# The attention loop of a two-layer diffusion block, written out in place of a loop with registers

## The reference, cut to what matters

```python
def attend_block(q_blk):                      # 128 queries at a time
    sc = jnp.einsum("bqhd,bkhd->bhqk", q_blk.astype(jnp.float32), k_all) * scale
    p = jax.nn.softmax(sc, axis=-1)
    return jnp.einsum("bhqk,bkhd->bqhd", p, v_all).astype(q_blk.dtype)
```

## Time and profile before

| what | us |
|---|---|
| median of 3 runs | 2488.7 |
| lowest and highest | 2485.72, 2490.02 |
| the profiled execution, its own time | 2494.57 |
| span of the profiled execution | 2492.7 |

### The profile page before, as it was taken

One profiled execution on the slowest core, in us unless ns is written; L12 is line 12 of the kernel. 1 busy time (PEld: TensorE's weight loads), 2 busy tenths in 40 slices (PEclk: granted clock), 3 DMA queues, 4 the chain that ended last, 5 costly groups with the idle time before them and its releaser, 6 DMA issues.

```text
span 2492.7 us, 32113 instructions
## 1 busy us (share of the span) xinstructions
PE 2418.2 (97%) x11124; PEld 1955.7 (78%) x11124; DVE 1848.6 (74%) x2786; ACT 1208.3 (48%) x1948; POOL 611.2 (25%) x473
## 2 busy tenths in 40 slices
PE   8989999999899999999999899999999999999997
PEld 3868878788788788888888687766887888888886
DVE  4467667677637988888754779998579888887556
ACT  3356656566643544444553442244635454445542
POOL 0057587864042300011000321100432000110002
PEclk9999999999999999999999999999999999999999
DMA  6046465642431455555865567711314555558644
GB/s 269 27 144 174 128 176 161 186 135 68 144 125 65 121 146 147 132 132 140 261 216 172 183 186 180 158 39 46 118 52 127 149 139 135 136 140 275 210 169 170
DMA packets 153204, 366.31 MB, mean 147 GB/s; under 512 B 14433, under 2 KB 15713, under 8 KB 153057
## 3 DMA queue, kind: packets, MB, share of 16 engines
q1 hardware_dynamic: 107056, 242.69, 28.1%
q0 software_dynamic: 44416, 116.93, 21.7%
q10 hardware_dynamic: 1584, 4.85, 0.6%
HBM read 303.07 MB, written 136.31 MB: 176 GB/s over the span
## 4 chain that ended last, share of the span: by engine, by line
PE 75%; DVE 18%; issue 4%; ACT 1%; DMA 1%; POOL 1%; SPq 0%; DVEq 0%; POOLq 0%; ACTq 0%
PE psum L2299 22%; PE psum L2301 22%; PE psum L2300 22%; DVE acts L2209 3%; DVE acts L2211 3%; PE psum L2515 2%; PE psum L2504 1%; PE psum L2505 1%; DVE small L1748 1%; DVE weights_f32r L1848 1%; DVE acts L2213 1%; DMA low<-x_t 1%; PE psum L2613 1%; DVE high_f32r L1966 1%; DVE low L1945 1%
## 5 line engine op out<-in xcount | busy, mean ns | idle before, releaser
L2299 PE MATMUL psum<-acts_f32r,weights_f32r 128*128 128x512 f32 x1536 | 607.8, 396 | 16.0 <-DVE low L2027 6.7
L2301 PE MATMUL psum<-acts_f32r,weights_f32r 128*128 128x512 f32 x1536 | 600.8, 391 | 0.0
L2300 PE MATMUL psum<-acts_f32r,weights_f32r 128*128 128x512 f32 x1536 | 600.2, 391 | 0.0
L955 ACT ACTIVATE weights_f32r<-low 128x512 fp32r<-128x512 f32 (+2 forms) x471 | 303.7, 660 | 447.5 <-DVE low L1994 257.4
L2299 PEld LDWEIGHTS psum<-acts_f32r,weights_f32r 128*128 128x128 f32 x1536 | 289.9, 189 | 80.2 <-DVE low L2027 7.5
L2301 PEld LDWEIGHTS psum<-acts_f32r,weights_f32r 128*128 128x128 f32 x1536 | 289.6, 189 | 61.3
L2300 PEld LDWEIGHTS psum<-acts_f32r,weights_f32r 128*128 128x128 f32 x1536 | 290.0, 189 | 58.6 <-issue 0.5
L862 POOL TENSOR_TENSOR low<-low 128x512 f32<-128x512 f32 x91 | 134.0, 1474 | 706.8 <-ACT low L1194 700.6
L2299 PE MATMUL psum<-high_f32r,weights_f32r 128*128 128x512 f32 (+1 forms) x485 | 191.8, 396 | 2.0 <-issue 2.0
L2300 PE MATMUL psum<-high_f32r,weights_f32r 128*128 128x512 f32 (+1 forms) x485 | 186.3, 384 | 0.0
L2301 PE MATMUL psum<-high_f32r,weights_f32r 128*128 128x512 f32 (+1 forms) x485 | 186.3, 384 | 0.0
(11 more groups left out here) (254 smaller groups left out, 4700.3 us busy)
## 6 DMA issues: line engine op xcount, KB each, us to landing
low<-units SPq DMA_DIRECT2D x130, 512.0 KB, 4.2
set<-mod_w POOLq DMA_DIRECT2D x80, 512.0 KB, 3.9
low<-gated_sums SPq DMA_DIRECT2D x110, 256.0 KB, 4.5
low<-weight_sums SPq DMA_DIRECT2D x88, 256.0 KB, 4.1
gated_sums<-low SPq DMA_DIRECT2D x22, 768.0 KB, 3.5
low<-units SPq DMA_DIRECT2D x66, 256.0 KB, 4.9
weight_sums<-units POOLq DMA_DIRECT2D x14, 1024.0 KB, 10.0
residual<-low SPq DMA_DIRECT2D x48, 256.0 KB, 2.0
```

Source lines behind the costliest of these rows:

```text
L955: return act.activation(out, in_, ACT.Copy, scale=scale)
L2299: pe.matmul(out, wl, xh, start=first, stop=False, skip_group_check=continued)
L2300: pe.matmul(out, wh, xl, start=False, stop=False, skip_group_check=continued)
L2301: return pe.matmul(out, wh, xh, start=False, stop=last, skip_group_check=continued)
```

## The change

PE, ACT and DVE no longer loop. `half_steps` itself calls the twelve half steps 2 to 13, with Python integers for `n` and `i`, so that each wait is on a constant. The order of instructions on each engine's datapath is the same. `Chain` loses the parts that served the loop.

```diff
@@ class Chain
     def __init__(self, engine, sem):
-        self.engine, self.sem, self.n, self.term = engine, sem, 0, 0
+        self.engine, self.sem, self.n = engine, sem, 0
 
     def __call__(self, ins):
         ins.then_inc(self.sem, 1)
         self.n += 1
-        self.engine.wait_ge(self.sem, self.term + self.n)
+        self.engine.wait_ge(self.sem, self.n)
...
-    def enter(self, i, per):
-        self.start, self.per, self.term = self.n, per, i * per
-
-    def leave(self, trips):
-        assert self.n - self.start == self.per, (self.n - self.start, self.per)
-        self.n, self.term = self.start + trips * self.per, 0
@@ def half_steps(step)
             step(0, 0, 0, turned=False, weighed=False)
             step(1, 1, 0, weighed=False)
-            yield 3
+            for i in range(3):
+                for q in range(2, 6):
+                    step(4 * i + q, q, i)
             step(14, 2, 3)
@@ ACT (PE the same)
-            for trips in half_steps(step):
-                with act.Fori(0, trips) as i:
-                    for q in range(2, 6):
-                        step(4 * i + q, q, i)
+            half_steps(step)
@@ DVE
-            for trips in half_steps(step):
-                with dve.Fori(0, trips) as i:
-                    chain.enter(i, 96)
-                    for q in range(2, 6):
-                        step(4 * i + q, q, i)
-                    chain.leave(trips)
+            half_steps(step)
```

## The result

| | before | after |
|---|---|---|
| median of 13 runs, us | 2488.7 | 2503.7 |
| lowest and highest | 2479.6, 2499.7 | 2493.2, 2508.9 |
| the profiled execution, and its span | 2494.6, 2492.7 | 2502.8, 2501.0 |

The ratio of after to before is 1.006, with a 95% interval of 1.0047 to 1.0073. The forecast was 2480.6 us, faster. The range ended at 2487.0.

What follows compares the result with a forecast made beforehand. PE, busy 97% of the span, was taken to bound the kernel, with POOL's blocks next. Gains of 1.3 + 6.8 + 0 = 8.1 us off the 2488.7 us median gave 2480.6 us, range 2472.5 to 2487.0.

Steps and rivals of the forecast that it cites:

- The branches, 15.15 us: Half steps 6 and 10: DVE's two taken backward branches cost 6.86 and 8.29 us, all removed; low end 7.28 us.
- The register arithmetic at 0: Attention loop: removing the register arithmetic for the waits gains 0 us, at the other end 0.1 us over 12 half steps.
- There are two parallel paths, and the longer decides: Between PE's modulation sums of successive trips: PE's path 118.4 and 117.1 us, POOL's 123.6 and 119.5 us; POOL's decides.
- A gain of only 1.3 us: Half step 4 to 8: PE waits 5.2 us for POOL, its sums take 7.72 us; 3.1 us gain at full clock.
- forecast gain of 8.1 us: Whole kernel: 1.3 us from half step 4 to 8, 6.8 us from 8 to 12, 0 after.
- Both at 123.6: Low bound of the POOL case: POOL's path 123.6 us in both trips, with clock loss, gains 4.0 us.
- if POOL's path depends on something that moves with PE: POOL's path in attention: named as one of the simplest ways for the prediction to be wrong; no size given.
- The forecast gain of 6.8 us in trip 3: Half step 8 to 12: 126.3 us today becomes POOL's 119.5 us, longer than PE's 117.1 us.
- nothing of the change is left: Beyond half step 12: no further gain or loss, 0 us; work behind attention moves forward as a whole.
- slower, by instruction fetch: Attention: PE must fetch some 12 more code packets, late ones stopping PE directly; kernel at 2498.0 us; chance 0.05.
- gaps of PE by issue at regular distances: Profile after: PE idle gaps ended by "issue", the sign that instruction fetch slows the kernel; no size given.

Runs made afterwards that it cites:

- third_acc: The changed kernel with three accumulators taking turns for POOL's blocks, each block waiting for the sums three blocks before; 2484.1 us, ratio 0.9976 to the kernel before.
- third_dve: The kernel before with only DVE's loop written out and a third accumulator for POOL's blocks; 2469.1 us, ratio 0.9932.
- dve_alone: The kernel before with only DVE's loop written out, PE and ACT keeping their loops; 2487.4 us, ratio 1.0002.
- spin_sized: The changed kernel with 34 and 26 dummy matmuls ahead of PE's wait for POOL in half steps 8 and 12; 2497.5 us, ratio 1.0027 to the kernel before.
- before_again: The kernel before, run once more without an edit; one run, 2484.1 us.
- thin_all: The changed kernel with weight sums on every fifth part of POOL's blocks instead of every third, 8 moved behind; 2490.5 us, ratio 1.002 to the kernel before.

## Why the prediction was wrong, step by step

**The branches, 15.15 us: right in kind.** Half steps 6 and 10 went to 30.3 to 31.6 us wherever DVE was written out. None of these kernels has a trace of the stand-still of 5.8 us there. The size is that of one execution; the second profile of before has 11.1 us. The register arithmetic at 0: right.

**"There are two parallel paths, and the longer decides": right as a mechanism.** The stops stand at L2319 in half steps 8 and 12, released by POOL's last addition, as I wrote. The third accumulator, which takes away only this wait, brings back 17 to 20 us (third_acc against after, third_dve against dve_alone).

**"A gain of only 1.3 us" in half step 8: the size was wrong, even with POOL's path near the forecast.** dve_alone is the case I had costed: its path was 125.7 us, 2 us over the 123.6. Its stop was 7.28 us, against my 5.2. The sums took 11.15 us (413.91 to 425.06), against my 7.72, which I had taken from a half step in which the low clock covered only part of them. And the low clock went on behind them. Half step 8 took 46.7 us where I had 41.6 (26.7 to the sums, 5.2 of stop, 7.7 for the sums and 2.0 behind them, 293.15 - 291.12 as in half step 4), and half step 9 took 31.9 for 30.3: 6.7 us more in all. spin_sized shows that the clock's part hangs on the standing still: with matmuls in its place the clock stayed at full speed. These 6.7 us leave 1.4 of the forecast gain of 8.1 us, and dve_alone measured no change (ratio 1.0002, with 0.2% to either side).

**"Both at 123.6": the bound of POOL's path was too short, and this is the step that failed.** I took its range from the two trips of the looped kernel, though I had written that the prediction falls "if POOL's path depends on something that moves with PE". It does: written out on PE, it is 125.9 to 130.6 us in trip 2 and 121.0 to 123.6 in trip 3, on average some 4 us more in each. What grows is POOL's waiting for transfers: from 430 to 550 us its idle time that ends with the landing of a mod_w part is 13.0 and 12.6 us in the two profiles of the kernel after, and 9.4, 7.5 and 7.7 in before, before_again and dve_alone. In the profiled execution the forecast gain of 1.3 us in trip 2 became a loss of 8.2: 5.9 us of it are the path (129.5 for 123.6) and 3.4 the sums (11.1 for 7.7). The forecast gain of 6.8 us in trip 3 became 2.5.

**Behind attention "nothing of the change is left": wrong.** The stretch takes 1 to 10 us longer in the written-out kernels, 5 in the profiled execution, where most of it is two stops at the "down" stages, where a fetch of PE's code now falls beside the loads that PE is about to need. In third_acc, the longest with 1909.1 us, PE's idle time in the stretch adds up to 37.6 us, against 30.2 in third_dve, and the granted clock is 0.50 for 36.1 us, against 33.0.

**The rival "slower, by instruction fetch": right in its sign, wrong in its place.** I looked for PE itself to stop ("gaps of PE by issue at regular distances"); there are none in attention. PE never waits for its own code there. It is transfers of other queues that come later, and PE waits for these through POOL and through DVE. By the Trainium skill, page Runtime: NRT & Kernel Launch, section Instruction fetch mechanics, crossing into the next block is "mostly hidden". For PE's own instruction stream this case agrees. For the kernel as a whole written-out code did cost time, 15 us between third_acc and third_dve; that the fetches are what costs it is shown for the two stops behind attention only.

**What stays open.** Why a fetch delays other transfers. Its 16 KB alone do not do it: 39 packets of that size left POOL's path where it was. It may be which engine they run on, how the instruction queue is served, or that a fetch starts together with something else of PE's. That the fetches themselves and nothing else of the written-out PE lengthen POOL's path is not shown either; that it goes with them is (6 to 7, 11, and 16 to 18 fetches), and for the two stops the place of the fetch decides. Against it stand thin_all, with 17 fetches and 119.2 us in trip 3, and the landings in spin_sized. No run writes out ACT alone, and none gives the kernel before a third accumulator while all its loops stay.

## What to carry to other kernels

Before a stall is taken out, follow the nearest parallel path to its end, and give its length the spread of several executions and room for a change that moves it; here 3 us of slack stood against 7 us of gain. A stop of PE can cost more than itself: 7.3 us of standing still took another 7.4 of clock. Write out a loop on the engine whose branch costs time (DVE), not on all of them for symmetry, and take away the wait that comes next in the same step: the first alone gave nothing (ratio 1.0002), both together 0.7%, the change as it was made minus 0.6%.

## What the runs showed of the hardware that I had not expected

Two backward branches of DVE, of 63 ns at most, were followed by 5.76 and 5.92 us in which the engine stood still, and in a second execution by 5.57 and 4.59. ACT, which loops too, showed no such stand-still.

Where a packet of PE's instruction queue (16,384 bytes, 1.03 us) began less than 12 us ahead of one of the two places at the start of the "down" stages, PE stopped there for 0.9 to 3.3 us; where none did, for 0.66 us at most. Transfers of 512 KB that met such a packet landed after 5.7 to 6.5 us in six kernels, against 4.4 to 4.7 for the others, but in spin_sized (5.2 us) and thin_all (4.9) no later than chance gives. Ordinary packets of 16,372 bytes (0.61 us) did little or nothing.

PE's loop body of four half steps was not fetched again in its second and third pass (no packet from 324 to 591 us). Where the fetches of a long straight program fall moved with the instructions ahead of them: 106 small matmuls more in attention removed two stops of 3 us, some 700 and 1,700 us later.
